# Products of the memory heads from high and low parts in a one-core streaming encoder layer

## The reference, cut to what matters

```python
A = jnp.exp(D - mt[..., None]) * jnp.einsum('bthd,bshd->bhts', qb, kb)
num = (jnp.einsum('bhts,bshe->bthe', A, vb)
       + jnp.moveaxis(iw, 1, 2)[..., None] * jnp.einsum('bhed,bthd->bthe', C, qb))
...
C_new = dec[..., None, None] * C + jnp.einsum('bhs,bshe,bshd->bhed', sw, vb, kb)
n_new = dec[..., None] * n + jnp.einsum('bhs,bshd->bhd', sw, kb)
```

## Time and profile before

| | |
|---|---|
| median of three runs | 1730.23 us (1728.5 to 1730.5) |
| the profiled execution, its time | 1730.19 us |
| its span in the trace | 1728.4 us |
| TensorE, matmuls | 1720.4 us, 100% of the span |
| VectorE | 906.1 us, 52% |
| ScalarE | 654.4 us, 38% |
| GpSimd | 405.2 us, 23% |
| DMA | 295.18 MB, mean 171 GB/s |

### The profile page before, as it was taken

The page is one execution under the profiler, slowest core; times in us unless marked ns, Lnnn a source line. Parts: engine busy times, 40 slices in busy tenths (PEclk is TensorE's granted clock), DMA queues, the critical chain, the costliest instruction groups (busy, mean ns, idle before and its releaser), DMA issues.

```text
span 1728.4 us, 24600 instructions
## 1 busy us (share of the span) xinstructions
PE 1720.4 (100%) x8414; PEld 1467.0 (85%) x8414; DVE 906.1 (52%) x1669; ACT 654.4 (38%) x1224; POOL 405.2 (23%) x596
## 2 busy tenths in 40 slices
PE   9999999999999999999999999999999999999999
PEld 8999999999987888888888888887888888888887
DVE  5634776556687666545433554343465334456333
ACT  5324754444344444333332333232333332333332
POOL 2721010002451353433000343000343100234100
PEclk9999999999999999999999999999999999999999
DMA  7775479999998687665444565444556444556543
GB/s 191 204 170 151 127 173 213 218 207 216 250 256 260 155 219 204 177 186 159 125 131 122 166 184 175 130 125 124 160 166 182 141 130 122 164 165 171 173 144 97
DMA packets 295939, 295.18 MB, mean 171 GB/s; under 512 B 97184, under 2 KB 202716, under 8 KB 295836
## 3 DMA queue, kind: packets, MB, share of 16 engines
q1 hardware_dynamic: 255606, 222.91, 47.0%
q0 software_dynamic: 25168, 67.06, 14.8%
q10 hardware_dynamic: 15062, 3.86, 1.2%
HBM read 261.51 MB, written 38.02 MB: 173 GB/s over the span
## 4 chain that ended last, share of the span: by engine, by line
PE 97%; DVE 2%; issue 0%; DMA 0%; ACT 0%; ACTq 0%; DVEq 0%
PE bank L675 9%; PE bank L634 9%; PE bank L676 9%; PE bank L635 9%; PE bank L633 9%; PE bank L674 9%; PE acc L535 8%; PE acc L537 7%; PE acc L536 7%; PE bank L2075 3%; PE ssb L633 2%; PE ssb L634 2%; PE ssb L635 2%; PE ssb L674 2%; PE ssb L675 2%; PE ssb L676 2%
## 5 line engine op out<-in xcount | busy, mean ns | idle before, releaser
L515 DVE TENSOR_TENSOR w_lo<-raw,w_hi 128x512 fp32r<-128x512 f32 x768 | 537.9, 706 | 754.4 <-ACT w_hi L506 753.8
L506 ACT ACTIVATE w_hi<-raw 128x512 fp32r<-128x512 f32 x768 | 482.8, 631 | 958.5 <-PE acc L537 194.9
L535 PE MATMUL acc<-a_hi,w_hi 128*128 128x400 f32 (+1 forms) x768 | 267.6, 348 | 0.2 <-DVE w_lo L515 0.2
L536 PE MATMUL acc<-a_lo,w_hi 128*128 128x400 f32 (+1 forms) x768 | 263.1, 343 | 0.0
L537 PE MATMUL acc<-a_hi,w_lo 128*128 128x400 f32 (+1 forms) x768 | 262.6, 342 | 0.0
L614 POOL DMA_DIRECT2D u_turned<-m x192 | 123.8, 652 | 552.3 <-DVE m L2018 552.0
L675 PE MATMUL bank<-w_lo,a_hi 128*128 128x512 f32 x640 | 253.2, 396 | 0.0
L633 PE MATMUL bank<-w_hi,x2g_hi 128*128 128x512 f32 x640 | 252.2, 394 | 1.0 <-issue 1.0
L634 PE MATMUL bank<-w_lo,x2g_hi 128*128 128x512 f32 x640 | 253.0, 395 | 0.0
L676 PE MATMUL bank<-w_hi,a_lo 128*128 128x512 f32 x640 | 252.8, 395 | 0.0
L635 PE MATMUL bank<-w_hi,x2g_lo 128*128 128x512 f32 x640 | 252.5, 394 | 0.0
(11 more groups left out here) (351 smaller groups left out, 1819.8 us busy)
## 6 DMA issues: line engine op xcount, KB each, us to landing
raw<-in_w_up SPq DMA_DIRECT2D x128, 512.0 KB, 3.8
raw<-in_w_down SPq DMA_DIRECT2D x128, 512.0 KB, 3.8
raw<-in_w_in SPq DMA_DIRECT2D x94, 512.0 KB, 4.7
raw<-in_w_out SPq DMA_DIRECT2D x32, 512.0 KB, 5.4
u_turned<-m POOLq DMA_DIRECT2D x192, 64.0 KB, 2.9
stage<-u_turned POOLq DMA_DIRECT2D x16, 768.0 KB, 6.1
vc<-in_cache_v POOLq DMA_DIRECT2D x32, 256.0 KB, 7.3
kc<-in_cache_k SPq DMA_DIRECT2D x128, 64.0 KB, 3.6
```

The lines of the kernel that those rows point to most:

```text
L506: e.activation(w_hi[:, q], raw[:, slot, 4 * (q % 2):4 * (q % 2) + 4, :], ACT.Copy).then_inc(hi_ready, 1)
L515: e.tensor_tensor(w_lo[:, q], raw[:, slot, 4 * (q % 2):4 * (q % 2) + 4, :], w_hi[:, q].bitcast(F32), ALU.subtract).then_inc(lo_ready, 1)
L535: e.matmul(out, w_hi[:, q, kk], hi[:, k, at], start=k == 0, stop=False, skip_group_check=True)
L536: e.matmul(out, w_hi[:, q, kk], lo[:, k, at], start=False, stop=False, skip_group_check=True)
```

## The change

Numerators of blocks 1 and 2 and the three large products of cp are made from high and low parts. ScalarE rounds values and scaled keys at slot 2 of a head (kv_hi) and the weighed exponents at slot 4 (expo_hi); GpSimd makes the low parts of values and keys, first of its work in each head; VectorE the low part of the weights (expo_lo). The parts lie in new tiles, two of them in the space of og_abs and h_rows. The first numerator block and the running streams' products stay native. The weighing comes at slot 2 of every head; it was at slot 3 in heads 0 and 1. kv_blk has one buffer, and the next head's blocks are loaded behind GpSimd's subtraction of the present head; the gates of head 1 are loaded after that too. The state normalisers and stream masks (n_blk, bmask and what is made from them) are loaded and prepared at tile T_AV = 16 and no longer when the heads start. The residual blocks are split at later quarters. Two semaphores are merged into others (gw_padded, bias_ordered).

```diff
-HEAD_AT = (("rows", 0), ("decay", 0), ("scores", 1), ("expo", 1), ("ksw", 1), ("weigh", 3), ("cn", 4),
+HEAD_AT = (("rows", 0), ("decay", 0), ("scores", 1), ("expo", 1), ("ksw", 1), ("weigh", 2), ("kv_hi", 2),
+           ("expo_hi", 4), ("expo_lo", 4), ("cn", 4),
            ("take0", 4), ("take1", 5), ("take2", 5), ("take3", 6), ("num", 6), ("hsum", 6), ("cp", 7), ("og", 7),
...
-            if what == "weigh" and h >= 2:
-                at -= 1
...
             if t == T_MLP:
-                return [(8, 9, 10, 11), (), (), ()][q]
+                return [(), (8, 9), (10, 11), ()][q]
             if t == T_MLP + 2:
-                return [(12, 13), (14, 15), (), ()][q]
-            return {(T_OUT2 + 4, 1): (0, 1), (T_OUT2 + 4, 3): (2, 3), (T_OUT2 + 6, 1): (4, 5), (T_OUT2 + 6, 3): (6, 7)}.get((t, q), ())
+                return [(), (12, 13), (14, 15), ()][q]
+            return {(T_OUT2 + 5, 1): (0, 1), (T_OUT2 + 5, 3): (2, 3), (T_OUT2 + 6, 3): (4, 5), (T_OUT2 + 7, 1): (6, 7)}.get((t, q), ())
...
-            e.memset(kv_blk[0:32, 1, 3, :, TAIL:32], 0.0).then_inc(S("v_blk_padded"), 1)
             load_C(0)
             load_mo(0)
-            load_v_blocks(1)
-            load_mo(1)
             for h in range(NH):
 
+                if h:
+                    done(e, ("cp", h - 1))
+                e.wait_ge(S("head_hi"), 2 * h + 1)
+                e.tensor_tensor(v_lo[:], v_rows[:, 1:4], v_hi[:].bitcast(F32), ALU.subtract).then_inc(S("kv_lo"), 1)
+                e.tensor_tensor(k_swp_lo[:], k_swp[:], k_swp_hi[:].bitcast(F32), ALU.subtract).then_inc(S("kv_lo"), 1)
+                if h + 1 < NH:
+                    e.wait_ge(S("v_turned"), h + 1)
+                    load_v_blocks(h + 1)
+                if h == 0:
+                    load_mo(1)
                 read_out(e, ("cn", h, 3))
...
                 if h + 2 < NH:
 
-                    e.wait_ge(S("v_turned"), h + 1)
-                    load_v_blocks(h + 2)
                     read_out(e, ("hT", 0, h), ("hT", 1, h))
                     load_mo(h + 2)
...
+                    elif what == "kv_hi":
+                        e.wait_ge(S("k_swp_made"), h + 1)
+                        e.activation(v_hi[:], v_rows[:, 1:4], ACT.Copy)
+                        e.activation(k_swp_hi[:], k_swp[:], ACT.Copy).then_inc(S("head_hi"), 1)
+                    elif what == "expo_hi":
+                        read_out(e, ("sx", h), ("sy", h))
+                        if h:
+                            e.wait_ge(S("og_log"), h)
+                        e.activation(expo_hi[:], expo[:, P:], ACT.Copy).then_inc(S("head_hi"), 1)
...
                     elif what == "rows":
                         if h:
                             done(e, ("cp", h - 1))
-                        e.wait_ge(S(f"v_blk_in{h % 2}"), 16 * 13 * (h // 2 + 1))
+                            e.wait_ge(S("kv_lo"), 2 * h)
+                        e.wait_ge(S("v_blk_in"), 16 * 13 * (h + 1))
...
+                    elif what == "expo_lo":
+                        read_out(e, ("sx", h), ("sy", h))
+                        e.wait_ge(S("head_hi"), 2 * h + 2)
+                        if h:
+                            done(e, ("hT", 1, h - 1))
+                        tt(expo_lo[:], expo[:, P:], expo_hi[:].bitcast(F32), ALU.subtract).then_inc(S("expo_low"), 1)
...
+            def in_parts(out, held, rows, first, last):
+
+                (held_hi, held_lo), (rows_hi, rows_lo) = held, rows
+                mm(out, held_hi, rows_hi, first, False)
+                mm(out, held_hi, rows_lo, False, False)
+                return mm(out, held_lo, rows_hi, False, last)
+
             def numerators(h):
-                read_out(e, ("sx", h), ("sy", h))
-                e.wait_ge(S("v_turned"), h + 1)
+                e.wait_ge(S("kv_lo"), 2 * h + 1)
+                e.wait_ge(S("expo_low"), h + 1)
...
                 b = fill(e, ("num", 1, h))
-                mm(b[:, 0:DVX], expo[:, P:2 * P], v_rows[:, 1], True, False)
-                filled(mm(b[:, 0:DVX], expo[:, late:late + P], v_rows[:, 2], False, True), ("num", 1, h))
+                in_parts(b[:, 0:DVX], weights(P), values(1), True, False)
+                filled(in_parts(b[:, 0:DVX], weights(late), values(2), False, True), ("num", 1, h))
...
             def new_rest(h):
                 b = fill(e, ("cp", h))
+                e.wait_ge(S("kv_lo"), 2 * h + 2)
                 for r in range(1, 4):
-                    mm(b[:, 0:DVX], k_swp[:, r - 1], v_rows[:, r], r == 1, r == 3)
+                    in_parts(b[:, 0:DVX], (k_swp_hi[:, r - 1], k_swp_lo[:, r - 1]), (v_hi[:, r - 1], v_lo[:, r - 1]), r == 1, r == 3)
```

More of the change, by code:

```diff
@@ L365, in build @@
         gate_b = sb("gate_b", [NH, 2])
+        bmask = sb("bmask", [P, BD])
+        n_blk = sb("n_blk", [P, BD * NH])
+        nT = sb("nT", [P, BD, NH])
+        swm = sb("swm", [P, NH, BD])
+        bpair = sb("bpair", [P, 6])
+        swp = sb("swp", [P, NH, 2])
         with ExitStack() as s:
@@ L407, in build @@
             iwB = sb("iwB", [P, NH, NS], scope=s)
+            with ExitStack() as s_n:
+                expo_lo = sb("expo_lo", [P, 5 * P], F32R, scope=s_n)
             h_rows = sb("h_rows", [P, 3, DV], scope=s)
@@ L818, in _ @@
                 for r in range(4):
-                    dma(row_cols[0:ROWS[r], r], gate_cols(2, 2 * NH, STARTS[r], ROWS[r]), "ml_in")
+                    dma(row_cols[0:ROWS[r], r], gate_cols(2, 2 * NH, STARTS[r], ROWS[r]), "row_in")
                 for x, at in enumerate((NPR, META, META + P)):
-                    dma(emcol[:, x], gate_cols(4, NH, at, P), "ml_in")
+                    dma(emcol[:, x], gate_cols(4, NH, at, P), "row_in")
+            for j in range(4):
+                dma(n_blk[32 * j:32 * j + 32], bass.AP(tensor=state_n.tensor, offset=32 * j, ap=[[DQ, BD * NH], [1, 32]]),
+                    "row_in")
+            dma(bmask[:], seq_of_row, "row_in")
             for n in range(16):
@@ L1606, in take_av @@
                 taken(e.tensor_copy(av_rows[0:TAIL, 3, cs], b[0:TAIL, 3 * P:4 * P]), ("av", n))
+            e.wait_ge(S("row_in"), 16 * 12)
+            e.transpose(nT[:].rearrange("p b h -> p (b h)"), n_blk[:]).then_inc(S("seq_paired"), 1)
+            tt(bpair[:, 0:4], bmask[:, 0:4], bmask[:, 4:8], ALU.add).then_inc(S("seq_paired"), 1)
+            e.wait_ge(S("seq_paired"), 2)
+            tt(bpair[:, 4:6], bpair[:, 0:2], bpair[:, 2:4], ALU.add).then_inc(S("seq_paired"), 1)
+            e.wait_ge(S("seq_paired"), 3)
+            for h in range(NH):
+                ts(swp[:, h], bpair[:, 4:6], cols[:, 1, 0, h:h + 1], None, ALU.mult)
+                last = ts(swm[:, h], bmask[:], cols[:, 1, 0, h:h + 1], None, ALU.mult)
+            last.then_inc(S("seq_paired"), 1)
+            e.wait_ge(S("seq_paired"), 4)
             e.wait_ge(acc_free, T_AV)
@@ L1892, in enter @@
                 e.memset(expo[:, EXPO_LATE:EXPO_LATE + P - META], 0.0)
-                tt(bpair[:, 0:4], bmask[:, 0:4], bmask[:, 4:8], ALU.add).then_inc(S("seq_paired"), 1)
-                e.wait_ge(S("seq_paired"), 2)
-                tt(bpair[:, 4:6], bpair[:, 0:2], bpair[:, 2:4], ALU.add).then_inc(S("seq_paired"), 1)
-                e.wait_ge(S("seq_paired"), 3)
-                for h in range(NH):
-                    ts(swp[:, h], bpair[:, 4:6], cols[:, 1, 0, h:h + 1], None, ALU.mult)
-                    last = ts(swm[:, h], bmask[:], cols[:, 1, 0, h:h + 1], None, ALU.mult)
-                last.then_inc(S("seq_paired"), 1)
-                e.wait_ge(S("seq_paired"), 4)
             def head_work():
@@ L2119, in _ @@
                 if k == KT // 2 - 1:
[L2120 removed]
+                    e.wait_ge(S("consts"), 5)
                     e.wait_ge(S("diag_made"), 2)
```

68 lines of the change are left out of this document (33 added, 35 removed).

## The result

The changed kernel takes 1732.39 us (median of 22 runs, 1730.35 to 1733.92), the kernel before 1729.86 us in the same session: a ratio of 1.0014, 95% interval 1.0008 to 1.0020. It is slower by about 2.5 us, where 2.9 us less were forecast, and lies outside the range. The profiled execution took 1730.35 us with a span of 1728.5.

What follows compares the result with a forecast made beforehand. TensorE, busy 1720.4 of 1728.4 us, bounds the kernel. Gains of 2.32 us (products in parts) and 0.59 (earlier weighing), all else 0, take 1730.19 to 1727.3 us; range 1726.0 to 1729.4.

Steps and rivals of the forecast that it cites:

- Part 1: Eight fp32 products a head become three single-pass products each, at 117 ns: 0.58 us a head gained, 2.32 us in four heads.
- the state's rest: Three products of the new state in each head, made from parts: 1.05 us against 1.30, a gain of 0.25.
- the seam: TensorE's return from native fp32 to single-pass work, about 0.19 us lost: taken as moved, 0; bounds 0.19 gained, 0.1 lost a head.
- Part 2: Weighing one slot earlier in heads 0 and 1: TensorE's wait in head 0 goes, 0.59 us gained.
- Rival (c): No gain from parts: short products bound at 139 ns, only the earlier weighing's gain left, 1729.6 us; chance 0.06.
- rival (b): Faster than forecast by over 0.2%, at the range's low end, 1726.0 us; its reasoning is not in the text; chance 0.20.
- The tight spot: Head 1: GpSimd's subtraction queued behind the gates' load, low part done near 493.4, numerators at 494.1 just met; 0 taken.
- Part 3: New rounding and subtractions on ScalarE, VectorE and GpSimd: hidden beside the projection stream, cost 0; head 1 bound 1.2 us.
- rival (a): The gates' landing holds GpSimd in head 1, TensorE waits 1.2 us at the numerators: 1728.5 us; chance 0.20.
- the gates' term: TensorE's wait in head 1 for GpSimd's subtraction behind the gates' load: taken as 0, bound 1.2 us.
- Part 4: Earlier stream-factor loads and masks, one block buffer in place of two, later residual blocks: each 0.

## Why the prediction was wrong

**Right, by its own steps.** Part 1: 0.58 us a head forecast; measured 0.18 in the numerators (1.91 against 2.09), 0.23 in the state's rest (1.07 against 1.30) and 0.19 at the seam, 0.60 in all. The sum was right with two terms mis-sized that nearly cancel, which is luck: the spacing is 120 ns and not 117, with 0.23 us for the first step (1.91 us, not 1.76), and the seam had been set to 0. The return behind the numerators now costs nothing, 0.19 gained, and what the return in front of the parts costs is inside the first step, 0.23 where the others take 0.12. Part 2: 0.59 forecast; the wait is gone (0.63 less at that place in the changed kernel's trace), and putting the slot back costs 1.1 us in head 0 and 0.6 in head 1. In the version where the gates' landing plays no part, the heads' stages are 2.88 us shorter than before (149.38 against 152.26), where 2.91 were forecast. Rival (c), with 139 ns, fell at the 120. No run shows the pace behind rival (b), whose 1726.0 us is the low end of the range; the runs show the 120 ns in its place.

**The tight spot.** Part 3 named the right place and the right cause (the gates' landing ahead of v_lo in head 1) and then took 0 on a margin of nothing. Its price, 1.2 us, was for a wait that no trace has, so that it resembles the cost by the medians is chance. GpSimd's v_lo takes 1.56 us, not 2.3, and TensorE never waited at the numerators as rival (a) has it. The delay goes another way, through VectorE, whose expo_lo (3.10 us for 0.81) or split of the weights (2.7 to 2.9 for 0.69) is held up beside the two subtractions, to its reading of the last tile's sum and so to the output projection. A split of 1.35 us beside a subtraction of GpSimd was among the rows of before, but the forecast's sum has no term for such a hold-up, here 2.2 us beside two of them, nor for what stands behind it on VectorE. With the gates' term at its bound the forecast would have been 1728.5, and in the changed kernel's trace, where it is 0.22 us, it would still have looked unneeded.

**Part 4, "Each 0", failed twice.** First, the masks at tile 16: the step asked whether the data were there (they were, 60 us early) and not what stands behind the masks on VectorE. n_lo does, in the row that the forecast quotes, and TensorE waits 0.35 us for it; the stage takes 0.63 us more. Second, and 4.35 us of the 5: the step priced the early loads, the masks and the block buffer by when they are done, and where they push the other tiles it did not ask. They push x2g_hi and x2g_lo by 480 bytes, the held tiles of 2304 products on the path, and each product is 1.9 ns slower. No row of the trace of before shows this cost; the rows of the up-projections show only that they are 31% of the time without a wait, so a change in their step, however small, counts 2304 times. No rival was a slower main stream.

**The account**, from the forecast's 2.9 us gain to the 2.5 us loss, 5.4 us: x2g's place 4.35, the masks 0.63, late landings about 1.2, together 6.2. The 0.8 too much is within what sessions differ by; the 1.2 is the term known least, and the pause of 1.1 us that some executions have is not in the sum. All three removed: 1726.24 us, 6.15 under the changed kernel by medians of two sessions, 0.34% by the two ratios.

## What to carry to other kernels

When a change adds or moves a buffer, write down the addresses of the tiles behind it that feed the long matmul streams, before and after: a shift of 32 bytes cost 4 us here in stages that the diff doesn't touch. For work moved to an earlier place, ask not only whether its inputs are there, but which instruction stands behind it on its engine and who waits for that one. Keep short work that others depend on out of a queue behind a wait for a DMA landing: it cost 0.22 us in the profiled execution and about 1.2 in the median. And where an instruction may be held up, ask for the last thing behind it on its engine that another engine needs, not only for its own result.

## What the runs showed of the hardware

- The step of 512-column products went with the distance between the addresses of the held and the moving tile: 231.4 to 231.9 ns in the mean over a usual stage where it is a multiple of 64 bytes (133.30 to 133.55 us for 576 products), 233.1 to 233.4 where it is 32 off (134.27 to 134.44). With both tiles moved by 32 bytes together an up-projection took 133.34 us, with neither 133.35. The sum of three steps of 400 columns hardly reacted: 547.2 ns before, 547.6 and 547.8 with one tile of the pair off.
- VectorE's subtraction of 640 columns (expo_lo) takes 0.81 us alone, 1.90 to 2.20 where it ended 0.7 us behind the first of GpSimd's two subtractions, and 3.10 where it ended 0.7 us behind the second; that of 512 columns takes 0.69 alone and 2.7 to 2.9 beside two.
- GpSimd's subtraction of 774 columns takes 1.56 us, that of 384 takes 1.0 to 1.6: a price worked out by the column from the 1.15 us of such a one before (2.3 us) is too high.
